# A two-layer hybrid decoder trunk in fp32: earlier accumulating transfers, weight blocks one per step, and bias rows added by GpSimd

## The reference, cut to what matters

```
x  = layer_norm(alpha * x + mix @ w_out, ln1_g, ln1_b)
up = x @ w_up                                     # 1088 x 5632
hc = conv_b + sum(conv_w[i] * hp[:, i:i+T])       # causal, width 3, depthwise
g, u = hc[:, :2816], hc[:, 2816:]
y  = (gelu(g) * u) @ w_down                       # 1088 x 1024
x  = layer_norm(alpha * x + y, ln2_g, ln2_b)
```

## Time and profile before

| | us |
|---|---|
| median of 3 runs | 2557.95 |
| lowest, highest | 2546.45, 2564.44 |
| the profiled execution, its time | 2561.84 |
| its span | 2560.1 |
| PE busy | 2222.9 (87%) |
| DVE, ACT, POOL busy | 1609.4, 1044.0, 930.9 |

### The profile page before, as it was taken

One profiled execution on the slowest core, in us unless ns is written; L12 is line 12 of the kernel. 1 busy time (PEld: TensorE's weight loads), 2 busy tenths in 40 slices (PEclk: granted clock), 3 DMA queues, 4 the chain that ended last, 5 costly groups with the idle time before them and its releaser, 6 DMA issues.

```text
span 2560.1 us, 35253 instructions
## 1 busy us (share of the span) xinstructions
PE 2222.9 (87%) x13868; PEld 1989.6 (78%) x13868; DVE 1609.4 (63%) x2064; ACT 1044.0 (41%) x1867; POOL 930.9 (36%) x554
## 2 busy tenths in 40 slices
PE   7999998888788887599899999989889888876996
PEld 7987678888788885478788866789888887854875
DVE  1569668666665665355836686777566665662557
ACT  3227565333333334245522375553333333341543
POOL 1134255454444542301221334555444444332112
PEclk9999999999899998799999999999989999987998
DMA  6221462444444448969651215614434444599695
GB/s 167 67 52 36 126 187 77 113 106 105 106 111 104 103 102 261 273 168 221 165 153 43 56 32 161 195 63 112 106 94 119 103 116 100 127 274 263 160 212 155
DMA packets 257468, 338.92 MB, mean 132 GB/s; under 512 B 39184, under 2 KB 157712, under 8 KB 257232
## 3 DMA queue, kind: packets, MB, share of 16 engines
q1 hardware_dynamic: 222424, 261.69, 32.7%
q0 software_dynamic: 34880, 74.98, 17.7%
HBM read 217.65 MB, written 98.03 MB: 123 GB/s over the span
## 4 chain that ended last, share of the span: by engine, by line
PE 31%; DVE 17%; POOL 16%; DMA 16%; issue 10%; ACT 8%; SPq 1%; ACTq 0%; POOLq 0%; DVEq 0%
DMA e_scr<-hg 11%; PE ps L2718 10%; PE ps L2306 8%; DMA araw<-a_scr 5%; POOL wblk L973 4%; POOL wblk L969 3%; PE ps L2565 3%; POOL bl L961 3%; DVE hg L1878 2%; DVE hg L1875 2%; POOL wblk L980 2%; POOL wblk L977 2%; ACT hg L1311 2%; PE ps L2626 2%; ACT bh L1274 1%
## 5 line engine op out<-in xcount | busy, mean ns | idle before, releaser
L2626 PE MATMUL ps<-bt,bh 128*128 128x272 f32 (+1 forms) x3520 | 629.7, 303 | 152.4 <-ACT gu L1283 137.2
L2626 PEld LDWEIGHTS ps<-bt,bh 128*128 128x128 f32 x3520 | 535.6, 202 | 162.3 <-ACT gu L1283 145.9
L2626 PE MATMUL ps<-bt,bl 128*128 128x272 f32 (+1 forms) x1760 | 384.4, 300 | 0.0
L1274 ACT ACTIVATE bh<-wblk 128x512 fp32r<-128x512 f32 x308 | 181.5, 622 | 490.5 <-POOL wblk L973 283.9
L2718 PE MATMUL ps<-dh,ah 128*128 128x512 f32 x616 | 257.9, 419 | 100.7 <-DVE al L1918 98.4
L961 POOL TENSOR_TENSOR bl<-wblk,bh 128x512 fp32r<-128x512 f32 x98 | 160.3, 1638 | 427.4 <-ACT bh L1274 427.4
L2626 PEld LDWEIGHTS ps<-bt,bl 128*128 128x128 f32 x1760 | 295.2, 201 | 0.0
L2718 PE MATMUL ps<-dl,ah 128*128 128x512 f32 x616 | 252.0, 409 | 0.0
L2718 PE MATMUL ps<-dh,al 128*128 128x512 f32 x616 | 251.3, 408 | 0.0
L2626 PE MATMUL ps<-ba,bh 128*128 128x272 f32 (+2 forms) x1408 | 235.6, 289 | 16.3 <-DVE gu L1864 14.6
L1841 DVE TENSOR_TENSOR bl<-wblk,bh 128x512 fp32r<-128x512 f32 x210 | 165.0, 819 | 124.0 <-ACT bh L1274 124.0
(11 more groups left out here) (260 smaller groups left out, 4444.4 us busy)
## 6 DMA issues: line engine op xcount, KB each, us to landing
wblk<-in_w_up SPq DMA_DIRECT2D x88, 512.0 KB, 5.3
a_scr<-hg SPq DMA_DIRECT2D x44, 552.0 KB, 3.2
e_scr<-hg POOLq DMA_DIRECT2D x44, 512.0 KB, 7.0
araw<-a_scr SPq DMA_DIRECT2D x66, 256.0 KB, 8.4
araw<-e_scr SPq DMA_DIRECT2D x66, 256.0 KB, 6.1
w<-in_w_down POOLq DMA_DIRECT2D x16, 1024.0 KB, 16.6
wrow<-in_w_out SPq DMA_DIRECT2D x48, 256.0 KB, 5.1
wrow<-in_w_out SPq DMA_DIRECT2D x24, 512.0 KB, 4.5
```

The costliest lines, as they stand in the source:

```text
L1274: act.activation(bh[b][:], block_of(f, b), ACT.Copy).then_inc(S["u_hi"], 1)
L2626: e = nc.tensor.matmul(up_half(f, b, n), lhs, rhs[:, c:HW_] if n else rhs[:, 0:c], start=(k == 0 and m == 0), stop=(k == HK - 1 and m == 2))
```

## The change

1. In the up stage POOL issues `act_add` case 0 (odd f) or case 1 (even f) right behind its two low parts, ahead of the sums of f, and case 2 behind the third sum, ahead of S3.
2. In the down stage SP loads `w21`, `w22` and `w12` in single blocks (128 x 512, 256 KB), one in each of the steps 4 to 36, each waiting until the block before the last has landed (`wb0`, `wb1`); the residual tiles, gains, and the negations and sums of T_1, T_3, T_4 move in the order with them.
3. The bias rows are added by POOL instructions: one in `residual` behind the multiplication (nine tiles), in place of R_8, R_TOP and R_BOT, and one in `gained` in place of its transfer (six tiles).

The diff, cut to its core:

```
@@ sync
+            def down_block(l, i):
+                n, k = divmod(i, KP)
+                tile, c = ((w21, 0), (w22, HT), (w12, HT))[n]
+                if i >= 2:
+                    sp.wait_ge(S[f"wb{i % 2}"], wb_count(l, i - 2))
+                src = w_down[l].rearrange("(k two p) n -> two p k n", two=2, p=P)[1]
+                sp.dma_start(tile[:, k, :], src[:, k, c:c + HT]).then_inc(S[f"wb{i % 2}"], 16)
...
                 for s in range(4, NST):
                     if s == 4:
                         gains(l, 0)
                         gains(l, 1)
                         z_back(l, NB)
-                    elif s in (5, 7):
+                    elif 5 <= s < 9:
+                        if s == 6:
+                            sample_raw(l, 2)
                         z_back(l, s - 5)
-                        z_back(l, s - 4)
-                    elif s == 6:
-                        sample_raw(l, 2)
-                        down_block(l, "w21", 0, 0, 6)
-                    elif s == 8:
-                        down_block(l, "w21", 1, 6, KP)
...
-                    elif s == 12:
-                        down_block(l, "w12", 2, 8, KP)
-                    elif s in (14, 16):
-                        if s == 14:
-                            sp.wait_ge(S["adds1"], 16 * KP * (l + 1))
-                        z_back(l, s // 2 - 3 + (s - 14) // 2)
-                        z_back(l, s // 2 - 2 + (s - 14) // 2)
-                    elif s == 15:
-                        sp.wait_ge(S["sm_lo"], 4 * (l + 1))
-                        down_block(l, "w12", 0, 0, 4)
-                    elif s == 17:
-                        down_block(l, "w22", 0, 0, KP)
                     elif s == 18:
                         conv_rows(l, NRB - 1)
-                    elif s == 21:
+                    elif 20 <= s < 24:
+                        if s == 20:
+                            sp.wait_ge(S["adds1"], 16 * KP * (l + 1))
+                        z_back(l, s - 16)
+                    elif s == 26:
+                        sp.wait_ge(S["sm_lo"], 4 * (l + 1))
                         sp.wait_ge(S["neg"], neg_t(l, T_1, 0) + 1)
-                        down_block(l, "w12", 1, 4, 8)
-                    elif s == 26:
+                    elif s == 38:
                         sp.wait_ge(S["e_out"], 16 * KP * (l + 1))
                         sp.wait_ge(S["f_out"], 16 * KP * (l + 1))
                         gains(l, 2)
                         gains(l, 3)
+                    if s < 4 + 3 * KP:
+                        down_block(l, s - 4)
                     act_block(l, s)
@@ gpsimd
                 pool.tensor_tensor(rz, rz, gain[0][0:q, :], ALU.mult).then_inc(S["xp"], 1)
+                pool.wait_ge(S["xp"], xp_n(l, t) + 1)
+                pool.tensor_tensor(rz, rz, gain[1][0:q, :], ALU.add).then_inc(S["xp"], 1)
...
                 pool.wait_ge(S["n_ym"], n + 1)
-                after(pool, "n_yp", 16 * n)
-                pool.dma_start(rz, gain[3][0:q, :], accum_op=ALU.add).then_inc(S["n_yp"], 16)
+                pool.tensor_tensor(rz, rz, gain[3][0:q, :], ALU.add).then_inc(S["n_yp"], 1)
...
                 for f in range(1, FT):
                     lo_up(l, f, B_11)
                     lo_up(l, f, B_12)
+                    if f >= 3:
+                        act_add(l, (f - 3) // 2, 1 - f % 2)
                     for b in SUMS[:3]:
                         sum_up(l, f, b)
-                    sum_up(l, f, B_S3)
                     if f >= 5 and f % 2:
                         act_add(l, (f - 5) // 2, 2)
-                    if f >= 3 and f % 2:
-                        act_add(l, (f - 3) // 2, 0)
-                    elif f >= 4:
-                        act_add(l, (f - 4) // 2, 1)
+                    sum_up(l, f, B_S3)
                 act_add(l, KP - 2, 1)
                 residual(l, NB)
-                residual_add(l, R_8)
                 act_add(l, KP - 2, 2)
                 act_add(l, KP - 1, 0)
-                weight_add(l, T_1, 0)
                 for t in range(4):
                     residual(l, t)
                 act_add(l, KP - 1, 1)
-                residual_add(l, R_TOP)
+                weight_add(l, T_1, 0)
+                act_add(l, KP - 1, 2)
+                residual_add(l, R_P1)
                 weight_add(l, T_1, 1)
-                act_add(l, KP - 1, 2)
                 weight_add(l, T_1, 2)
-                residual_add(l, R_P1)
                 for t in range(4, NB):
                     residual(l, t)
-                residual_add(l, R_BOT)
@@ scalar
                     elif s == 4:
                         scaled_gains(l)
-                        weight_neg(l, T_1, 0)
...
                     elif s == 8:
                         sample_hi(l, 3)
-                        weight_neg(l, T_1, 1)
+                        weight_neg(l, T_1, 0)
...
-                    elif s == 11:
-                        weight_neg(l, T_1, 2)
+                    elif s in (12, 15):
+                        weight_neg(l, T_1, s // 3 - 3)
...
-                    elif s in (36, 37, 38):
-                        weight_neg(l, T_3, s - 36)
-                    elif s in (40, 41, 42):
-                        weight_neg(l, T_4, s - 40)
+                    elif s in (36, 38, 40):
+                        weight_neg(l, T_3, s // 2 - 18)
+                    elif s in (41, 42, 44):
+                        weight_neg(l, T_4, (41, 42, 44).index(s))
```

More of the change, by code:

```diff
@@ L75 @@
 RESID = [8, 0, 1, 2, 3, 4, 5, 6, 7]
-R_8, R_TOP, R_P1, R_BOT, R_U2T, R_U2B, R_U2C, RADDS = 1, 2, 3, 4, 5, 6, 7, 7
+R_P1, R_U2T, R_U2B, R_U2C, RADDS = 1, 2, 3, 4, 4
 KGRP = [(0, 4), (4, 8), (8, KP)]
@@ L152, in xp_n @@
 def xp_n(l, t):
[L154 removed]
+    return 2 * (l * len(RESID) + RESID.index(t))
 def neg_a(l, k, which):
@@ L623, in up_cols, with first_blocks @@
                         .then_inc(S[f"wu_landed{f % 2}"], 16)
[L625 to L630, removed]
+            def first_blocks(l, n, k0, k1):
+                src = w_down[l].rearrange("(k two p) n -> two p k n", two=2, p=P)[0][:, k0:k1, 0:HT]
+                at_ = w12[:, 4 + k0:4 + k1, :] if k0 < 4 else w11[:, k0:k1, :]
+                sp.dma_start(at_, src).then_inc(S[f"wc_landed{n}"], 16)
+            def down_block(l, i):
[5 more added lines that the diff above has]
+                sp.dma_start(tile[:, k, :], src[:, k, c:c + HT]).then_inc(S[f"wb{i % 2}"], 16)
             def act_block(l, s):
@@ L1012, in residual_add @@
                 p1s = p1[:]
-                if which == R_8:
-                    pool.wait_ge(S["xp"], xp_n(l, NB) + 1)
-                    out, src = rzd[NB][0:NS, :], gain[1][0:NS, :]
-                elif which in (R_TOP, R_BOT):
-                    out = rz_top if which == R_TOP else rz_bot
-                    pool.wait_ge(S["xp"], xp_n(l, 3 if which == R_TOP else 7) + 1)
-                    out, src = out[:], gain[1][:].unsqueeze(1).to_broadcast([P, 4, D])
-                elif which == R_P1:
+                if which == R_P1:
+                    pool.wait_ge(S["xp"], xp_n(l, 3) + 2)
                     pool.wait_ge(S["p1_ev"], 4 * (l + 1))
@@ L1336, in weight_neg @@
                 elif which == T_3:
-                    act.wait_ge(S["w12"], 48 * (l + 1))
+                    for i in (2 * KP + k1 - 1, 2 * KP + k1 - 2):
+                        act.wait_ge(S[f"wb{i % 2}"], wb_count(l, i))
                     out, src = w12, w12[:, k0:k1, :]
@@ L1685, in sample_part @@
                 rz = half_of(NB, half)
-                dve.wait_ge(S["radd"], 16 * (RADDS * l + R_8))
+                dve.wait_ge(S["xp"], xp_n(l, NB) + 2)
                 if n:
@@ L1700, in join @@
                     dve.wait_ge(S["joins"], JOINS * l + {J_C22: J_VB, J_C21: J_P7}[j] + i + 1)
+                elif j == J_P3:
+                    dve.wait_ge(S["xp"], xp_n(l, t) + 2)
                 else:
-                    dve.wait_ge(S["radd"], 16 * (RADDS * l + {J_C11: R_P1, J_P3: R_TOP, J_VT: R_U2T, J_VB: R_U2B, J_P7: R_U2C}[j]))
+                    dve.wait_ge(S["radd"], 16 * (RADDS * l + {J_C11: R_P1, J_VT: R_U2T, J_VB: R_U2B, J_P7: R_U2C}[j]))
                 rz = half_of(t, half)
```

24 lines of the change are left out of this document (13 added, 11 removed), and 2 rows, old and new, of the table S.

## The result

The changed kernel took 2356.56 us, median of 4 runs (2351.85 to 2361.99), against 2557.91 us for the kernel before beside it: ratio 0.9218, 95% interval 0.9179 to 0.9257, so 7.8% faster. The profiled execution took 2361.99 us with a span of 2360.2.

What follows compares the result with a forecast made beforehand. It took the gate's wait for `act_add`'s transfer, 202.8 us, to hold the up stage. 2561.84 - 161 (up stage) - 18 (down stage) = 2382.8, less 3.9 gives 2379 us; own range 2330 to 2430, range with rivals 2300 to 2450.

Steps and rivals of the forecast that it cites:

- The wait disappears: Up stage: the gate's wait for the add's transfer, 5.34 us in each of 38 loops, goes but for the longest landings.
- The issue's 0.95 us: Up stage: issuing the add ahead of the sums costs POOL's path 0.95 us a loop, bounds 0 and 1.5.
- Row stores, +6: Up stage: 18 small stores on SP ahead of the next weights, in three f of each layer, cost 6 us.
- Gates 21 to 22.5 us apart, full clock: Sign of being right: up-stage gates at this spacing, with PE at full granted clock through the stage.
- Front, -18 a layer: Down stage, first third: a loss of 32 us in place of 50, so -18 per layer, bounds -35 and 0.
- Steps 4 to 20: Sign of being right, down stage: these steps take about 80 us instead of 101.
- the lower tiles' train: Down stage: POOL operations of the four lower tiles, partly under other waits, lose PE 11 us.
- Tail, +9 a layer: End of down stage: a second POOL operation in `gained` delays DVE, four intervals by 2.35 us, bounds 0 and 12.
- The slow issue: Rival, up stage: POOL's issue waits for a DVE convolution, 2.8 us in place of 0.95, giving 2449; 10%.
- The late store: Rival, up stage: the store of line 660 lands late and POOL waits before the sums, giving 2455; 9%.
- All of it hides: Rival: the issue costs nothing and the down stage gains 30 us a layer instead of 9, giving 2301; 9%.
- SyncE's wait pacing the steps: Rival, down stage: SP's wait for block i - 2 costs time from 6.3 us of landing; 2650 at 14 us; 5%.

Runs made afterwards that it cites:

- e1: The kernel before with only the new order of the up loop, the adds ahead of the sums: 2357.65 us, ratio 0.9221.
- e2: The changed kernel with the old order of the up loop, the adds back behind the last sum: 2553.15 us, ratio 0.998.
- e3: The changed kernel with all adds in GpSimd's idle gap, behind the third sum and ahead of S3: 2412.83 us, ratio 0.9439.
- e7: The changed kernel with one more 128x512 subtraction on GpSimd in each of the 42 up loops, ahead of the add: 2444.31 us, ratio 0.9565.
- e11: The changed kernel with the residual's bias (R_8, R_TOP, R_BOT) added by transfers again, single weight blocks kept: 2348.83 us, ratio 0.9183.
- e4: The changed kernel with the gained bias added by a transfer again: 2338.77 us, ratio 0.9146.
- e5: The changed kernel with the gained product and addition on GpSimd cut into halves of 512 columns, each waiting for the one before: 2334.3 us, ratio 0.9138.
- e6: The changed kernel with four single weight blocks under way instead of two: 2355.69 us, ratio 0.9215.
- e12: The kernel before with the new up loop order and the residual's bias on GpSimd, weight loads and gained pair as before: 2351.59 us, ratio 0.9194.
- e9: The changed kernel with residual and gained products and bias additions all in halves of 512 columns, each waiting for the one before: 2322.42 us, ratio 0.9078.

## Why the prediction was right, and where its terms were off

2379 was forecast, 2356.6 measured, inside the range of 2300 to 2450 and the forecast's own of 2330 to 2430. Its mechanism, the moved adds, carries the whole gain (e1, e2). The span fell by 200 where the sum had 179; the 21 us are -40 in the up stage, +10 in the fronts, +3 in the tails and the +6 ahead of the up stage, which is scatter. So the total is nearer than its largest term, because errors of both signs met.

*The wait disappears: right.* 202.8 us became 0. The landing fell from a median of 7.7 us to 5.8, which the prediction did not count. e3 shows that the place matters by the landing, as the prediction reckoned.

*The issue's 0.95 us: mis-sized, nothing of it seen in the time.* Of 38 x 5.34 = 203 us, 201 came. From 454 to 987 us before and 455 to 890 after, GpSimd's group of the first sum went from 2357 ns (19 times) to this:

```profile
L970 POOL TENSOR_TENSOR wblk<-wblk 128x512 f32<-128x512 f32 x19 | 33.4, 1760 | 0.0
L978 POOL TENSOR_TENSOR wblk<-wblk 128x512 f32<-128x512 f32 x20 | 25.8, 1292 | 3.2 <-POOL wblk L974 0.4
```

The second line, S4, was 1479 before; the sum between them (line 974) went from 2213 to 2267. So of the issue's 1.2 us some 0.6 + 0.2 came back in shorter sums, read here as turns with VectorE that fall otherwise (no run separates it), and VectorE's product fell too, from 1530 to 1351 ns on average. The rest, 0.4 us, does not show in the time, since the loop has TensorE's 21.15 us as its floor with it or without it. The prediction saw this turn and allowed it 0.25 to 0.55 us (1.2 to 1.5 down to 0.95). Its error was to charge the rest in full, though it named TensorE's 21.0 to 21.4 us as what is late next. e7 shows how near that edge is: by the estimate there some 0.2 us were left.

*Row stores, +6: mis-sized, about 0.* From 470 to 850 us, where two of the three stretches of 18 stores lie, TensorE was busy in all 380 us (the windows row below), and in 39.92 of the 40 us from 850 to 890, where the third lies.

*Gates 21 to 22.5 us apart, full clock: right.* Timeline of ScalarE, 714 to 745 us, and the windows view, 470 to 850 us (the last three columns are the granted clock, the DMA share and GB/s; 1.00 is the upper of the clock's two levels, 2.4 GHz):

```profile
718.84 1.31 ACT L1303 ACTIVATE hg<-gu,par 128x1104 f32<-128x1104 f32 x1
740.07 1.31 ACT L1303 ACTIVATE hg<-gu,par 128x1104 f32<-128x1104 f32 x1 [0.16 <-ACT gu L1291]
```

```profile
470.00:850.00 380.00, 380.00 (x3024) 379.18 (x3023) 296.47 (x327) 166.13 (x288) 194.80 (x134) 1.00 0.52 132
```

*Front, -18 a layer: -13.3 and -12.3, inside the bounds.* With the moved adds alone the fronts were already some 4 us shorter (159.6 to 155.8, 159.9 to 155.3), little more than the scatter. Steps 4 to 20, about 80 us forecast, took 75.3 (911.61 to 986.93), where before took 101.1. But 17.4 us followed up to the next step (to 1004.30), 6.6 before: the lower tiles' train, GpSimd's operations in a row, stood in the way, forecast at 11. The chain of 940 to 1010 us:

```profile
980.84 2.89 DVE dl L1907
983.73 2.81 DVE al L1911
```

A cost that none of its terms names: after a long wait TensorE's first step ran at the lower of its two clock levels, 1.2 GHz. Behind the wait of 9.13 us before 999.19, the mean granted clock was 0.56 from 999.0 to 1004.2 us and twelve matmuls took 5.04 us; behind 4.48 us before 906.03 it was 0.50 from 906 to 911 us. At full clock twelve took 2.72.

The reason given for the gain was half wrong. It counted the accumulating traffic removed as the larger relief, 24.5 of 38 us. By e11 the gain of the front is there without that relief, so it comes from item 2; and the additions that replace the transfers take their relief back.

*Tail, +9 a layer: +9.4 and +11.8.* Mechanism and size held, both low parts of a tile at 2.45 to 2.78 us, and e4 and e5 confirm the cause.

*The rivals.* The slow issue would have shown issues above 2.5 us; the longest took 1.56, though 38 of them ran beside a convolution, as the one at 705.09 with 1.23. (The Trainium skill, page "SBUF — State Buffer", section "SBUF: two separate sides", says that descriptors are held back while VectorE is in a 2-port perf mode; the traces do not name such a mode, so no run here tests it.) The late store would have left GpSimd idle ahead of its first sum or add; none of its rows there has such a wait. All of it hides: true of the issue, not of the down stage. SyncE's wait pacing the steps: part of its sign is there, 40 us of idle time in layer 1 and a longest landing of 17.1 us. Single blocks landed in 5.1 us at the median over both layers, but in 6.3 from 890 to 987 us, the very value from which the wait was to count. That it does not cost time is shown by e6.

## What to carry to other kernels

Issue a transfer that a later step waits for as soon as its data are there, ahead of work on the same queue that it does not need. Here the issue took 1.2 us of the queue and nothing that the time shows; the landing, 5.6 to 9.6 us, is what must be over. Where GpSimd works beside VectorE's operations with two SBUF inputs, the length of a single GpSimd operation sets what each of VectorE's costs: cut it before moving the work elsewhere. Here there was a wait between the pieces; pieces without one were not run. Two edits that relieve the same stretch are not worth their sum: item 2 and the removal of the residual's transfers took 16 and 15 us off the fronts when added up one by one (e11, e12 against e1), and 9.5 and 7.7 together. And an edit of the same change can cost what another brings: the down stage here held -27 and +25.

## What the hardware showed that was not expected

VectorE's low part of 128x512 took 0.68 us alone, mostly 2.45 to 2.90 us beside GpSimd operations of 1024 columns (2.4 to 2.8 us) and mostly 1.4 to 1.8 us beside those of 512 (1.3 to 1.8 us): it waits for the end of the one operation under way. The exception comes once in each layer of the changed kernel: at 915.25 us a low part took 7.36 us, past an addition, two issues and the multiplication behind them. GpSimd pays something for the cut: a half took 1.6 us at the median in e9, an operation of 1024 columns 2.7 in the changed kernel.

The price of work added on GpSimd was far from proportional: 2.1 us a loop for the first subtraction of about 1.9 us, 0.5 for the second. Turns with VectorE (a product of 1.30, 3.47 or 2.38 us at the same place) move as one list shifts against the other.
